# A 4-mixer transformer slice on one core: sums of the MLP weight quarters made by adding DMAs in DRAM

## The reference, cut to what matters

```python
def sq_relu_mlp(h, w_up, w_down):
    u = jnp.einsum('btd,df->btf', h, w_up)                         # [512,1024] x [1024,4096]
    return jnp.einsum('btf,fd->btd', jnp.square(jax.nn.relu(u)), w_down)

x = first_block(x, ...)          # layer 0: stick breaking, layer 1: latent attention (MLA)
for layer in range(2):           # second_block
    u = rms_norm_2(h, mix_norm_g[layer])
    h = h + (even_mixer if layer % 2 == 0 else diff_mixer)(u, ...)
    h = h + sq_relu_mlp(rms_norm_2(h, mlp_norm_g[layer]), mlp_w_up[layer], mlp_w_down[layer])
return rms_norm_2(h, final_norm_g)
```

## Time and profile before

| | us |
|---|---|
| median of 3 runs | 1832.42 (1831.35 to 1832.48) |
| the profiled execution | 1835.86 |
| its span | 1834.0 |
| PE busy | 1789.8 (98%) |
| DVE busy | 1150.3 (63%) |
| ACT busy | 866.9 (47%) |
| POOL busy | 450.9 (25%) |
| all DMA traffic | 149.20 MB, mean 81 GB/s |

### The profile page before, as it was taken

One profiled execution on the slowest core, in us unless ns is written; L12 is line 12 of the kernel. 1 busy time (PEld: TensorE's weight loads), 2 busy tenths in 40 slices (PEclk: granted clock), 3 DMA queues, 4 the chain that ended last, 5 costly groups with the idle time before them and its releaser, 6 DMA issues.

```text
span 1834.0 us, 26208 instructions
## 1 busy us (share of the span) xinstructions
PE 1789.8 (98%) x10340; PEld 1460.4 (80%) x10340; DVE 1150.3 (63%) x1861; ACT 866.9 (47%) x1409; POOL 450.9 (25%) x451
## 2 busy tenths in 40 slices
PE   7999999999999999999999999999999999999997
PEld 6877777775678757677879898988888787989896
DVE  5355556575546688854578575765677657858574
ACT  5236665455435465564345252633445434435253
POOL 0035551101311235560140000005678214000000
PEclk9999999999999999999999999999999999999999
DMA  5321111231013411111232322222222123232322
GB/s 177 101 78 49 47 47 58 80 101 50 24 47 100 133 60 34 36 36 58 80 122 86 115 93 104 93 97 83 84 88 76 46 81 127 81 115 92 106 91 80
DMA packets 44521, 149.20 MB, mean 81 GB/s; under 512 B 6000, under 2 KB 6384, under 8 KB 44400
## 3 DMA queue, kind: packets, MB, share of 16 engines
q1 hardware_dynamic: 44400, 147.53, 24.1%
HBM read 139.64 MB, written 2.10 MB: 77 GB/s over the span
## 4 chain that ended last, share of the span: by engine, by line
PE 85%; DVE 6%; ACT 4%; POOL 2%; issue 2%; DMA 1%; POOLq 0%; SPq 0%; DVEq 0%; ACTq 0%
PE BANK L301 18%; PE BANK L303 17%; PE BANK L302 17%; PE BANK L2405 4%; PE BANK L2404 4%; PE BANK L2402 4%; PE BANK L955 3%; PE BANK L688 2%; PE BANK L1739 1%; PE BANK L1720 1%; DMA WRAW<-in_wc 1%; DVE WL L278 1%; PE BANK L1696 1%; PE BANK L1012 1%; PE BANK L2710 1%
## 5 line engine op out<-in xcount | busy, mean ns | idle before, releaser
L269 ACT ACTIVATE WH<-WRAW 128x1024 fp32r<-128x1024 f32 (+1 forms) x214 | 223.0, 1044 | 340.8 <-PE BANK L303 306.0
L278 DVE TENSOR_TENSOR WL<-WRAW,WH 128x1024 fp32r<-128x1024 f32 (+1 forms) x201 | 256.3, 1276 | 138.8 <-ACT WH L269 138.6
L301 PE MATMUL BANK<-HH,WH 128*128 128x512 f32 x664 | 273.1, 411 | 12.1 <-DVE WL L278 9.8
L303 PE MATMUL BANK<-HL,WH 128*128 128x512 f32 x664 | 260.2, 392 | 0.0
L302 PE MATMUL BANK<-HH,WL 128*128 128x512 f32 x664 | 259.9, 391 | 0.0
L301 PE MATMUL BANK<-HIDH,WH 128*128 128x512 f32 (+1 forms) x520 | 201.2, 387 | 1.6 <-issue 1.5
L302 PE MATMUL BANK<-HIDH,WL 128*128 128x512 f32 (+1 forms) x520 | 200.7, 386 | 0.0
L303 PE MATMUL BANK<-HIDL,WH 128*128 128x512 f32 (+1 forms) x520 | 200.7, 386 | 0.0
L2405 PE MATMUL BANK<-HP,G 128*128 128x256 f32 x672 | 190.2, 283 | 0.0
L2404 PE MATMUL BANK<-HP,G 128*128 128x256 f32 x672 | 190.2, 283 | 0.0
L2402 PE MATMUL BANK<-HP,G 128*128 128x256 f32 x672 | 190.1, 283 | 0.0
(11 more groups left out here) (446 smaller groups left out, 3694.2 us busy)
## 6 DMA issues: line engine op xcount, KB each, us to landing
WRAW<-in_w SPq DMA_DIRECT2D x77, 512.0 KB, 3.5
WRAW<-in_wd SPq DMA_DIRECT2D x64, 512.0 KB, 3.5
RAW<-in_wf SPq DMA_DIRECT2D x32, 512.0 KB, 3.6
WRAW<-in_wu SPq DMA_DIRECT2D x16, 512.0 KB, 3.5
TMP<-in_wf SPq DMA_DIRECT2D x16, 512.0 KB, 3.5
WRAW<-in_w0o SPq DMA_DIRECT2D x8, 512.0 KB, 3.5
WRAW<-in_w1o SPq DMA_DIRECT2D x8, 512.0 KB, 3.4
WRAW<-in_wc SPq DMA_DIRECT2D x8, 512.0 KB, 3.5
```

Source lines behind the costliest of these rows:

```text
L269: e.activation(WH[b % NS][:, 0:n], WRAW[b % NR][:, 0:n], ACT.Copy).then_inc(*inc("s_high", ("high", b)))
L278: e.tensor_tensor(WL[b % NS][:, 0:n], WRAW[b % NR][:, 0:n], WH[b % NS][:, 0:n].bitcast(F32), ALU.subtract).then_inc(*inc("s_low_pool" if p ...
L301: e.matmul(dst, ah, bh, start=first and i == 0, stop=False)
L303: made = e.matmul(dst, ah, bl, start=False, stop=last and i == len(sets) - 1)
```

## The change: sums made by DMAs that add, ahead of their use

The four sums of a slot are no longer made by DVE. Two new inputs `first` and `second` hold copies of quarters in the order in which they are to be added (four slots of one half make a group `g`; 12 groups, six for each MLP). A scratch tensor `sums` of 2 MB for each group lies in DRAM. POOL starts all DMAs on it: step 0 copies 2 MB from `first`, step 1 adds 1 MB of `second` onto the first half, later steps add one part of `sums` (512 KB, in the groups of MLP 1 in two halves of 256 KB) onto the next. Since such a DMA can only add, the sums are of a form with additions alone, with some signs turned, and `plane_mix`, `join_first` and `join_last` turn theirs to match; `join_last` becomes two instructions of 256 columns. Each step waits, on POOL, until the step before it in its group has landed. `fast_load` now issues two DMAs: three quarters (384 KB) and the four sums (512 KB, in runs of 1 KB for MLP 0 and 2 KB for MLP 1).

```diff
@@ l0_gpsimd, ahead of the first low(...)
+            w.wait_ge(*at("evac", "l0g", 3))
+            for g, step in ((0, 0), (0, 1), (1, 0), (1, 1), (0, 2), (2, 0), (2, 1), (1, 2), (0, 3), (2, 2), (1, 3), (2, 3)):
+                sums_pool(e, w, g, step)
@@ l1_gpsimd, at its start
+            for g, step in ((3, 0), (3, 1), (4, 0), (4, 1), (3, 2), (5, 0), (4, 2), (3, 3)):
+                sums_pool(e, w, g, step)
@@ l2_gpsimd, at its start (and sums_pool(e, w, 5, 3) ahead of gelu_low(0))
+            for g, step in ((5, 1), (4, 3), (5, 2)):
+                sums_pool(e, w, g, step)
@@ mlp_gpsimd, at its end
+            if L == 0:
+                for g in range(6, 12):
+                    for step in range(6):
+                        sums_pool(e, w, g, step)
@@ fast_load, sums_pool
-            e.dma_start(raw_part(s, 0, 4), A[f"wf{L}"][s]).then_inc(*dma(f"s_raw{s % 3}"))
-
-        def fast_sums(e, w, L, s):
-            w.wait_ge(*dma(f"s_raw{s % 3}", L * NF // 3 + s // 3 + 1))
-            a21, a11, a12, a22, s1, s3, s2, s4 = (raw_part(s, i) for i in range(8))
-            e.tensor_tensor(s1, a21, a22, ALU.add).then_inc(*inc("s_fast_sum", ("first sum", L, s)))
-            e.tensor_tensor(s3, a21, a11, ALU.subtract).then_inc(*inc("s_fast_sum", ("third sum", L, s)))
-            w.wait_ge(*at("first sum", L, s))
-            e.tensor_tensor(s2, s1, a11, ALU.subtract).then_inc(*inc("s_fast_sum", ("second sum", L, s)))
-            w.wait_ge(*at("second sum", L, s))
-            e.tensor_tensor(s4, a12, s2, ALU.subtract).then_inc(*inc("s_fast_sum", ("sums", L, s)))
+            w.wait_ge(*sums_made(L, s))
+            g, i = 6 * L + s // 4, s % 4
+            e.dma_start(raw_part(s, 1, 3), A[f"wf{L}"][s]).then_inc(*dma(f"s_raw{s % 3}"))
+            e.dma_start(raw_part(s, 4, 4).rearrange("p (a b n) -> p a b n", a=2, b=2), sums_of(g)[:, :, :, i, :]).then_inc(
+                *dma(f"s_raw{s % 3}"))
+        def sums_pool(e, w, g, step):
+            sc = A["sums"][g]
+            if step:
+                w.wait_ge(*dma(f"s_sums{g}", step))
+            if step == 0:
+                e.dma_start(sc, A["first"][g]).then_inc(*dma(f"s_sums{g}"))
+                return
+            if step == 1:
+                e.dma_start(sc[:, 0:2048], A["second"][g], accum_op=ALU.add).then_inc(*dma(f"s_sums{g}"))
+                return
+            if g < 6:
+                dst, src = ((1, 0), (0, 0)) if step == 2 else ((1, 1), (1, 0))
+                e.dma_start(sums_of(g)[:, dst[0], dst[1]], sums_of(g)[:, src[0], src[1]], accum_op=ALU.add).then_inc(
+                    *dma(f"s_sums{g}"))
+                return
...
@@ join_last
-            e.tensor_tensor(Q[:, 0:4:3, :], Q[:, 5:7, :], pair_bank(pair, 3), ALU.add).then_inc(
+            e.tensor_tensor(Q[:, 3, :], half_bank(pair, 3, 1), Q[:, 6, :], ALU.subtract).then_inc(
+                *inc("s_joined", ("joined", *key, 5)))
+            e.tensor_tensor(Q[:, 0, :], Q[:, 5, :], half_bank(pair, 3, 0), ALU.add).then_inc(
                 *inc("s_joined", ("joined", *key, 3)))
```

More of the change, by code:

```diff
@@ L2277, in l2_gpsimd @@
             split("wc1", 1, 0)
+            sums_pool(e, w, 5, 3)
             gelu_low(0)
@@ new lines, in fast_load, with sums_made, sums_of @@
+            g, i = 6 * L + s // 4, s % 4
+            e.dma_start(raw_part(s, 1, 3), A[f"wf{L}"][s]).then_inc(*dma(f"s_raw{s % 3}"))
+            e.dma_start(raw_part(s, 4, 4).rearrange("p (a b n) -> p a b n", a=2, b=2), sums_of(g)[:, :, :, i, :]).then_inc(
+                *dma(f"s_raw{s % 3}"))
+        def sums_made(L, s):
+            return dma(f"s_sums{6 * L + s // 4}", 4 if L == 0 else 6)
+        def sums_of(g):
+            if g < 6:
+                return A["sums"][g].rearrange("p (a b i n) -> p a b i n", a=2, b=2, i=4)
+            return A["sums"][g].rearrange("p (a i b n) -> p a b i n", a=2, b=2, i=4)
@@ new lines, in sums_pool @@
+        def sums_pool(e, w, g, step):
[8 more added lines that the diff above has]
+                return
+            if g < 6:
+                dst, src = ((1, 0), (0, 0)) if step == 2 else ((1, 1), (1, 0))
+                e.dma_start(sums_of(g)[:, dst[0], dst[1]], sums_of(g)[:, src[0], src[1]], accum_op=ALU.add).then_inc(
+                    *dma(f"s_sums{g}"))
+                return
+            dst, src = ((1, 0), (0, 0)) if step < 4 else ((1, 1), (1, 0))
+            i = slice(2, 4) if step % 2 else slice(0, 2)
+            e.dma_start(sums_of(g)[:, dst[0], dst[1], i], sums_of(g)[:, src[0], src[1], i], accum_op=ALU.add).then_inc(
+                *dma(f"s_sums{g}"))
@@ L2338, in fast_high @@
         def fast_high(e, w, L, s):
-            w.wait_ge(*at("sums", L, s))
+            w.wait_ge(*dma(f"s_raw{s % 3}", 2 * (L * NF // 3 + s // 3 + 1)))
             if s > 2:
@@ L2365, in plane_mix @@
             w.wait_ge(*at("first mix", L, p))
-            e.tensor_tensor(S[:, 2, :], S[:, 5, :], S[:, 1, :], ALU.subtract).then_inc(
+            e.tensor_tensor(S[:, 2, :], S[:, 1, :], S[:, 5, :], ALU.subtract).then_inc(
                 *inc("s_mixed", ("second mix", L, p)))
             w.wait_ge(*at("second mix", L, p))
-            e.tensor_tensor(S[:, 3, :], S[:, 4, :], S[:, 2, :], ALU.subtract).then_inc(*inc("s_mixed", ("mixed", L, p)))
+            e.tensor_tensor(S[:, 3, :], S[:, 4, :], S[:, 2, :], ALU.add).then_inc(*inc("s_mixed", ("mixed", L, p)))
         def plane_high(e, w, L, p):
@@ L2427, in join_first @@
             w.wait_ge(*at("joined", *key, 1))
-            e.tensor_tensor(Q[:, 5:7, :], Q[:, 4:5, :].broadcast_to([128, 2, 256]), pair_bank(pair, 2),
-                            ALU.add).then_inc(*inc("s_joined", ("joined", *key, 2)))
+            e.tensor_tensor(Q[:, 5:7, :], pair_bank(pair, 2), Q[:, 4:5, :].broadcast_to([128, 2, 256]),
+                            ALU.subtract).then_inc(*inc("s_joined", ("joined", *key, 2)))
             w.wait_ge(*at("joined", *key, 2))
@@ L2511, in mlp_vector @@
                             fast_low(e, w, L, s + 2)
-                        if i < 5:
-                            fast_sums(e, w, L, s + 3)
                         if i > 5:
@@ L2529, in mlp_vector @@
                         fast_low(e, w, L, first + m - 5)
-                    if 3 < m < 7:
-                        fast_sums(e, w, L, first + m - 4)
             if L == 0:
@@ L3462, in quarters @@
         r = x.reshape(2, 4, 128, 2, 4, 128)[:, 2 * half:2 * half + 2, :, :, pair, :]
-        return np.ascontiguousarray(np.stack([r[0, :, :, 1], r[0, :, :, 0], r[1, :, :, 0], r[1, :, :, 1]]).transpose(
-            2, 0, 1, 3)).reshape(128, -1)
+        return np.stack([r[0, :, :, 1], r[0, :, :, 0], r[1, :, :, 0], r[1, :, :, 1]]).transpose(2, 0, 1, 3).reshape(128, 4, -1)
+    firsts, seconds = [], []
     def mlp(layer):
@@ L3468, in mlp @@
         first = add(f"wu{layer}", blocks(up[:, 0:1024]), [(("up", layer, 0), m) for m in range(8)])
-        fast = add(f"wf{layer}", [quarters(up[:, 1024 * c:1024 * c + 1024], pair, half) for c, pair, half in FAST],
-                   [("fast", layer, s) for s in range(len(FAST))])
+        parts = [quarters(up[:, 1024 * c:1024 * c + 1024], pair, half) for c, pair, half in FAST]
+        fast = add(f"wf{layer}", [x[:, 1:4].reshape(128, -1) for x in parts], [("fast", layer, s) for s in range(len(FAST))])
+        for g in range(0, len(FAST), 4):
+            four = np.stack(parts[g:g + 4], 1)
+            turn = (0, 2, 1, 3) if layer == 0 else (0, 1, 2, 3)
+            firsts.append(cat([four[:, :, k].transpose(turn).reshape(128, -1) for k in ([0, 0], [1, 2])], 1))
+            seconds.append(four[:, :, [3, 1]].transpose(turn).reshape(128, -1))
         down = add(f"wd{layer}", [b for c in range(4) for b in blocks(dn[1024 * c:1024 * c + 1024])],
@@ L3490, in lay_out @@
     plan += mlp(1)
+    arrays["first"], arrays["second"] = np.stack(firsts), np.stack(seconds)
     def col(v):
@@ L3511, in build @@
     A["plan"] = plan
+    A["sums"] = nc.dram_tensor("sums", arrays["first"].shape, F32).ap()
     o = nc.dram_tensor("out_x", (KT, 128, T), F32, kind="ExternalOutput").ap()
```

## The result

The changed kernel takes 1847.07 us, the median of 4 runs (1846.2 to 1849.23), beside 1832.45 us for the kernel before in 4 runs on the same chip (1831.35 to 1835.41): a ratio of 1.0079 [1.0062, 1.0096], 14.6 us slower. The forecast was 1847, some 15 us slower. The total came out as forecast, but most of it lies in another place than the forecast said, and has another cause: that the two numbers agree is luck.

The account below looks back on a forecast made before the run. PE's own pace was taken to bound the MLPs. Terms 0 + 0 + 0 + 13 (POOL late in layer 0) + 2 (clock) = +15 on 1832.4 gave 1847 us; range 1830 to 1864, the forecast's own 1836 to 1856.

Parts of the forecast that it names:

- DVE's relief: Slots of both MLPs: 81 us of DVE work removed, worth 0 (bounds 0 to -1.6 us), since PE has no idle time.
- The join in two, and the slots' loads: MLP slots: split join adds 0.16 us per pair, hidden; 896 KB load takes 4.8 us within 12.6; both cost 0.
- Layer 0, POOL 13 us late: Layer 0: twelve POOL DMAs need 84 us against 70.7 available, delaying PE's scores 13 us (bounds 0 and +45).
- factor k: POOL's DMAs within DRAM: cost of an added byte in copied bytes, taken as 1.75, bounded by 1 and 3.
- Layer 1, "hidden": Layer 1: POOL's copies and additions take 55 us (70 with k = 3) of 72.8 us, so cost nothing.
- rival 3: MLP 0: POOL's steps fit but the slots' loads starve, 13 us lost, 1845 us; chance 0.07.
- The clock: Behind PE's stop in layer 0: the granted clock falls, 2 us added; earlier dips cost at most 1.7 and 3.4.
- MLP 0: After MLP 0, POOL's 36 serial steps take 235 us (312 with k = 3) against 299.1: hidden, upper bound +13.
- A4: Theory from the experiments, not the prediction: two or more POOL transfers in flight starve the loads, whatever the piece size.
- Wrong: PE waiting for the low part of the slots: Sign against the forecast, pointing to rival 3: PE waits in the MLP slots for their low part.
- POOL free before 111 us: Sign against the forecast, pointing to rival 1: in layer 0 POOL is done before its first low plane is due.
- rival 1: POOL's steps fit and nothing changes (k below 1.24 in layer 0): 1832 us, 1830 to 1835; chance 0.37.

Follow-up runs that it names:

- the kernel with that wait: Changed kernel, 64 KB pieces kept, but in layer 1 each of POOL's DMAs waits until the one before has landed: 1837.47 us, ratio 1.0029.

## Why the prediction was right in its sum and wrong in its place

- **DVE's relief worth nothing: right.** 81 us were to go; DVE's busy time fell from 1150.3 to 1086.8, 64 us. The 81 were too large: of four sums in a row the starts stand only 0.33 to 0.46 us apart, so that their 0.42 us overlap and all 192 cover 72.7 us; another 6 of these overlap other work of DVE, and the split join adds 3.3. The kernel without POOL's DMAs runs at 1.0001. ACT's wait for DVE's sums is gone and has become one for PE (`G L2374 <- PE BANK L2435`, 102.3 us, with 20.8 us for the sums' loads beside it): ACT is ahead of PE, as read from the earlier trace rows.
- **The join in two, and the slots' loads, at 0: right.** In MLP 0, beside POOL's transfers, a slot's sums (512 KB) land in 7.5 us in `RAW` and 8.5 in `TMP` (medians): around the 7.8 that were allowed and inside the 12.6 of slack. The 6.5 of the page is over both MLPs; in MLP 1, with no such transfer, it is 5.3, above the 4.8 of the formula. PE is busy for 302.00 of 302 us in MLP 0.
- **Layer 0, POOL 13 us late: wrong, the step that failed.** POOL was done at 109.3, 1.8 us ahead of the bound, where the formula had it 13 us behind. The factor k was not at fault. One at a time, in layer 1 of the kernel with that wait, a copy takes 9.2 us from its issue to the next, and 1 MB of addition 8.2 and 9.95. Less the fixed 1.8 that is 283 GB/s for the copy and 164 and 129 for the additions, k = 1.7 and 2.2, around the 1.75 that was taken. Wrong was the 207 GB/s: I gave the loads their 99 GB/s first and POOL's transfers what was left. It went the other way. With all of 306 GB/s the same formula gives (6.29 + 5.24 x 1.75) / 0.306 + 9 = 59.5 us, and 64 with k = 2; it took 69 (39.97, where the first DMA was out, to 109.3). Solved for the rate, that is 15.5 / 60.3 = 256 GB/s, an estimate with k = 1.75. The 306 wasn't a ceiling either: windows of 10 us show 308 and 334 GB/s in layer 1. POOL's transfers held most of their rate, and the loads behind which PE waits landed late: 8 to 17.6 us in place of 3.5. Layer 0 still has loss, 2.7 us from the kernel without POOL's DMAs (114.90 to 117.58), through the same loads. That POOL can be late there is true, but it took smaller pieces (4 KB: 15.29 us of waiting).
- **Layer 1, "hidden": wrong, and the larger loss.** The window was held against POOL's transfers alone (55 of 72.8 us), and they did fit. The block loads of the same stretch were never priced. That is rival 3's mechanism (loads that starve), asked of the slots in MLP 0, where it didn't happen, and of no other place.
- **The clock: right in kind.** Behind stalls of 2.79 and 2.47 us the granted clock was 0.83 in two pieces of 10 us, at most 1.7 us each, as the earlier trace rows had it. It is part of the 10.3. Where a stall did come ahead of the scores, as forecast (4 KB pieces), the clock cost 2.8 us where 2 was taken.
- **MLP 0: right.** 36 steps in series, some 251 us (950.9 to about 1202) where the formula gave 235, POOL then idle for 48.2 us ahead of the odd mixer. In series there is one of POOL's DMAs in flight but for the five changes of group, where a copy is issued 0.7 us behind the last 256 KB addition; A4 says that one is harmless; ACT still waits up to 10.8 us for a down block there, and PE for none.
- **"Wrong: PE waiting for the low part of the slots"** did not occur, and "POOL free before 111 us" did. By the prediction's own test that was rival 1, no change, at 1832. The sum agrees with the forecast by luck: a cost that it left out (10.3 us in layer 1) was nearly as large as the one that it put in (13 in layer 0).

The rule on adding from the page "Collectives: The Full Stack" of the Trainium skill (half the rate of a copy) agrees with the trace: 164 and 129 beside 283 GB/s are 0.58 and 0.46 of it. The 207 to 214 GB/s for copies in HBM from its page "DMA: Bandwidth & Descriptors", section "Latency and other measured facts", are near the whole duration of a copy here, 2.10 MB in 9.2 us or 228 GB/s with the fixed part in it; the estimate of 45 us worked out from it failed by the same step as the forecast.

Still open: why a load of 512 KB takes 9 to 17 us beside two or three such transfers and about half of that beside one, when its own bytes need 1.7 us by the 306 GB/s. A DMA share of 0.97 to 1.11 in those pieces would fit engines that are simply full, but one at a time the share reaches 1.07 as well while loads issued in that window land in 5.6 to 6.8 us; and in MLP 0 one at a time gives a single landing of 16.3 us, where buffers absorb it. No run put plain copies in place of the additions, so whether adding matters for the landings isn't shown. Open as well is what holds POOL behind a copy of many pieces.

## What to carry to other kernels

- A background transfer is to be priced on both sides: whether it is done in time, and how late it makes each load that a busy engine waits for in the same stretch. Ask which loads have little slack there, not whether the average rate has room.
- Where two background chains can run side by side, let each transfer wait for the one before it, if the window allows it. Here this, with the steps dealt anew to the pauses, turned 1.0079 into 1.0011 with more bytes per us in layer 1.
- Taking 64 us off an engine that PE didn't wait for gave nothing (1.0001), so there was no gain to set against any cost.

## What the runs showed of the hardware

- A load of 512 KB that lands after 3.5 us took 8 to 17.6 us in the chain of waits beside two or three transfers within DRAM; in layer 1 the median was 11.6 us beside two or three, and 6.0 with one in flight at a time.
- Within DRAM, one at a time beside the kernel's loads in layer 1: 2 MB copied in 9.2 us, 1 MB added in 8.2 and 9.95, 512 KB in some 7.3.
- With 512 pieces of 4 KB in a copy, POOL was held 6 to 11 us at later DMAs in layers 0 and 1; with 256 pieces of 8 KB three times, 6.9 to 9.95 us; with 128 of 16 KB, or rows of 64 KB, not.
- Behind waits of PE of 3.73 to 15.29 us ahead of the scores (four kernels), the first 24 matmuls took 3.89 us, and 2.1 to 2.8 us were lost by the last matmul of line 688; behind waits of 0.97 to 1.86 us they took 2.18 to 2.20.
